# A two-block network on one core: the last gate's second half split into 160 and 96 columns

## The reference, cut to what matters

```python
def second_block(x, p, ...):
    ...
    for i in range(2):
        h = h + mix
        h = h + swiglu(rms_norm(h, norm_ffn[i]), ffn_w_in[i], ffn_w_out[i])
        gate = jax.nn.sigmoid(rms_norm(h, ple_norm[i]) @ ple_w_gate[i])
        h = h + gate * (p[i] @ ple_w_proj[i])
    return h
```

## Time and profile before

| | |
|---|---|
| runs, median (lowest to highest) | 1030.18 us (1029.44 to 1030.19) |
| the profiled execution's own time | 1030.42 us |
| its span, first to last instruction | 1028.5 us |
| TensorE busy in the span | 1021.3 us, 99% |
| VectorE, ScalarE, GpSimd busy | 84%, 64%, 7% |
| granted TensorE clock, mean | 1.000 |
| last matmul record starts | 1024.64 us |
| last transfer issued | about 1026.4 us |

### The profile page before, as it was taken

One profiled execution on the slowest core, in us unless ns is written; L12 is line 12 of the kernel. 1 busy time (PEld: TensorE's weight loads), 2 busy tenths in 40 slices (PEclk: granted clock), 3 DMA queues, 4 the chain that ended last, 5 costly groups with the idle time before them and its releaser, 6 DMA issues.

```text
span 1028.5 us, 17536 instructions
## 1 busy us (share of the span) xinstructions
PE 1021.3 (99%) x7069; PEld 934.7 (91%) x7069; DVE 861.6 (84%) x1072; ACT 657.4 (64%) x800; POOL 70.9 (7%) x53
## 2 busy tenths in 40 slices
PE   8999999999999999999999999999999999999998
PEld 8998999889999999888999999989888899999987
DVE  6888887689999978965899998777989699888874
ACT  5777545567666667765765656476876667555654
POOL 0000001200000030002005600010000200000010
PEclk9999999999999999999999999999999999999999
DMA  8746354655666646455465756555425466556651
GB/s 296 243 170 204 125 184 145 192 187 187 196 202 205 202 146 206 147 181 174 164 205 165 229 169 216 200 167 167 164 83 164 133 201 209 170 199 205 201 169 42
DMA packets 126657, 185.46 MB, mean 180 GB/s; under 512 B 3184, under 2 KB 97904, under 8 KB 126576
## 3 DMA queue, kind: packets, MB, share of 16 engines
q1 hardware_dynamic: 125984, 183.27, 54.0%
q0 software_dynamic: 160, 0.52, 0.2%
q10 hardware_dynamic: 432, 0.53, 0.2%
HBM read 183.26 MB, written 1.05 MB: 179 GB/s over the span
## 4 chain that ended last, share of the span: by engine, by line
PE 97%; DVE 1%; DMA 1%; issue 0%; ACT 0%; SPq 0%; DVEq 0%
PE PS L511 95%; PE PS L519 2%; DMA RAW<-in_w_in_dram 1%; DVE WL L2141 0%; DVE SC L2968 0%; DVE AR L2990 0%; DVE XT L3017 0%; SPq L3186 0%; DVE AR L2963 0%; DVE Z L3025 0%; DVE AR L2956 0%; DVE SC L2999 0%; ACT AR L1948 0%; DVE AR L2893 0%; ACT WH L1430 0%
## 5 line engine op out<-in xcount | busy, mean ns | idle before, releaser
L511 PE MATMUL PS<-Z,WH 128*128 128x256 f32 (+1 forms) x2608 | 484.4, 288 | 2.2 <-ACT WH L1430 1.7
L511 PEld LDWEIGHTS PS<-Z,WH 128*128 128x128 f32 x2608 | 407.8, 191 | 7.8 <-issue 1.6
L2134 DVE TENSOR_TENSOR WL<-RAW,WH 128x2048 fp32r<-128x2048 f32 (+4 forms) x174 | 354.1, 2041 | 51.1 <-ACT WH L1430 50.4
L511 PE MATMUL PS<-Z,WL 128*128 128x256 f32 x1352 | 370.9, 284 | 0.0
L511 PE MATMUL PS<-WH,Z 128*128 128x512 f32 (+1 forms) x1226 | 355.9, 366 | 0.3
L1430 ACT ACTIVATE WH<-RAW 128x2048 fp32r<-128x2048 f32 (+4 forms) x183 | 314.0, 1719 | 63.8 <-PE PS L511 52.5
L511 PEld LDWEIGHTS PS<-Z,WL 128*128 128x128 f32 x1352 | 255.5, 191 | 2.7
L511 PEld LDWEIGHTS PS<-WH,Z 128*128 128x128 f32 x1226 | 220.7, 189 | 37.1 <-issue 3.1
L511 PE MATMUL PS<-WL,Z 128*128 128x512 f32 (+1 forms) x613 | 222.2, 363 | 0.0
L511 PEld LDWEIGHTS PS<-WL,Z 128*128 128x128 f32 x613 | 116.0, 189 | 15.0
L511 PE MATMUL PS<-Z 128*128 128x512 f32 (+1 forms) x388 | 93.2, 388 | 0.0
(11 more groups left out here) (219 smaller groups left out, 766.1 us busy)
## 6 DMA issues: line engine op xcount, KB each, us to landing
RAW<-in_ffn_w_in_dram SPq DMA_DIRECT2D x44, 1024.0 KB, 5.2
RAW<-in_w_ff_dram SPq DMA_DIRECT2D x32, 1024.0 KB, 5.4
RAW<-in_ffn_w_out_dram SPq DMA_DIRECT2D x22, 1024.0 KB, 5.0
RAW<-in_w_in_dram SPq DMA_DIRECT2D x18, 1024.0 KB, 5.4
RAW<-in_gla_w_in_dram SPq DMA_DIRECT2D x12, 1024.0 KB, 5.3
RAW<-in_diff_w_in_dram SPq DMA_DIRECT2D x12, 1024.0 KB, 5.2
RAW<-in_ple_w_gate_dram SPq DMA_DIRECT2D x8, 1024.0 KB, 5.2
RAW<-in_w_out_dram SPq DMA_DIRECT2D x4, 1024.0 KB, 5.1
```

The source lines that it names most:

```text
L511: return e.matmul(o, l, r, start=start, stop=stop, skip_group_check=skip)
L2134: e.tensor_tensor(low, raw, high.bitcast(F32), ALU.subtract).then_inc(s["w_lo"], 1)
```

## The change

The second token block's last gate, 256 columns into bank 7, is made in two pieces: columns 0 to 159 into bank 7, then columns 160 to 255 into bank 3. The second piece waits for `ple_g` 5. Each piece has its own eight steps of three matmuls, its own sigmoid, its own product and sum, and its own transfer; the final wait is for six landings. The table `LAST_GATES` has a row for each piece: token block, first and last column, bank. Token block 0 stays whole.

```diff
+LAST_GATES = ((0, 0, 256, 6), (1, 0, 160, 7), (1, 160, 256, 3))
...
-        for tb in range(2):
+        for tb, n0, n1, bank in LAST_GATES:
+            if bank == 3:
+                e.wait_ge(s["ple_g"], 5)
             for k in range(8):
-                i = mm3(PS[:, 6 + tb, 0:256], [x[:, k, 128 * tb:128 * tb + 128] for x in ops],
-                        [x[:, k, :] for x in w], k == 0, k == 7)
-            i.then_inc(s["ple_t" if tb == 0 else "gemm"], 1)
+                i = mm3(PS[:, bank, 0:n1 - n0], [x[:, k, 128 * tb:128 * tb + 128] for x in ops],
+                        [x[:, k, n0:n1] for x in w], k == 0, k == 7)
+            i.then_inc(s["gemm" if bank == 3 else "ple_t"], 1)
...
-            for tb in range(2):
-                e.wait_ge(*((s["gemm"], c + 4) if tb else (s["ple_t"], 1)))
-                act(g[:, tb, 768:1024], PS[:, 6 + tb, 0:256], ACT.Sigmoid, scale=r[:, tb:tb + 1]).then_inc(s["ple_g"], 1)
+            for x, (tb, n0, n1, bank) in enumerate(LAST_GATES):
+                e.wait_ge(*((s["gemm"], c + 4) if bank == 3 else (s["ple_t"], x + 1)))
+                act(g[:, tb, 768 + n0:768 + n1], PS[:, bank, 0:n1 - n0], ACT.Sigmoid,
+                    scale=r[:, tb:tb + 1]).then_inc(s["ple_g"], 1)
...
-            for tb in range(2):
-                gated(8 + tb, tb, 768, 256)
+            for x, (tb, n0, n1, _) in enumerate(LAST_GATES):
+                gated(8 + x, tb, 768 + n0, n1 - n0)
...
-    for b in range(2):
-        e.wait_ge(s["ple_h"], 8 + b)
-        e.dma_start(o_rows[:, b, 768:1024], H[:, b, 768:1024]).then_inc(s["d_out"], 16)
-    e.wait_ge(s["d_out"], 80)
+    for x, (b, n0, n1, _) in enumerate(LAST_GATES):
+        e.wait_ge(s["ple_h"], 8 + x)
+        e.dma_start(o_rows[:, b, 768 + n0:768 + n1], H[:, b, 768 + n0:768 + n1]).then_inc(s["d_out"], 16)
+    e.wait_ge(s["d_out"], 96)
```

## The result

The changed kernel took 1032.12 us (median of 22 runs, 1031.11 to 1034.19), the kernel before 1030.21 us (22 runs, 1029.40 to 1032.23). The ratio is 1.0017, with a 95% interval of 1.0011 to 1.0023: 1.9 us by the medians, a small loss that the interval keeps apart from nothing. The forecast was 1032.0 us, plus 1.8. The profiled execution has a span of 1029.8 us; it reached the two pieces 0.53 us earlier than the profiled one before did, so times after 1021 us are compared as distances, not as they stand.

What follows compares the result with a forecast made beforehand. TensorE, busy 1021.3 of 1028.5 us, and the 3.56 us tail were taken as the bound. Plus 2.50 on TensorE less 0.68 in the tail gave plus 1.8 on 1030.18: 1032.0 us, range 1031.3 to 1032.8.

Steps and rivals of the forecast that it cites:

- TensorE's part: Matmuls of the two pieces: 48 at 0.112 us, 5.38 us instead of 2.88, so plus 2.50 us on the path.
- the last matmul's way through the array: Tail term: the last matmul, 160 columns narrower, passes through the array faster, minus 0.07 us.
- floor: Under every matmul on TensorE: its weight load sets at least 0.112 us, whatever columns it moves; given 65%.
- The tail: Last matmul, sigmoid, product, sum and transfer shrink by 160 columns: minus 0.68 us together, range minus 0.53 to minus 0.97.
- The wait: Second piece's wait for `ple_g` 5: the sigmoid it needs begins about 13 us earlier, so it costs nothing.
- the first piece's chain: First piece's sigmoid, product, sum and issue: under 1.65 us, hidden behind the second piece's 2.69 us of matmuls.
- the sixth transfer: The added transfer from splitting: the first piece's, 1.8 us at most, lands before the last one does, costing nothing.
- TensorE stays without gaps, so I leave the clock alone.: TensorE in the two pieces: granted clock stays at 1.00, the level of 2.4 GHz, so no clock cost was counted.
- By columns: Rival on TensorE: matmuls take 80 and 53 ns, minus 0.37 us, 1029.8 us; 12% together with a quicker float32r load.
- float32's pace: Rival on TensorE: float32r matmuls under 256 columns run as slowly as plain float32, 1037.3 to 1038.6 us; 17%.
- load and stream one after the other: Rival on TensorE: short streams can't cover the next load, pieces take 7.94 us, total 1034.6 us; 6%.
- quicker for float32r than for float32: Rival on TensorE: a quicker float32r weight load, result between by-columns and the forecast; 12% together with by-columns.

Runs made afterwards that it cites:

- half_load: The changed kernel, but its 96-column matmuls load 64 columns of weights instead of 128: 1030.88 us against 1030.23 for the kernel before.
- pe_only: Kernel before with only the matmuls split into 160 and 96 columns, both in bank 7, no wait, sigmoid to transfer whole: 1032.87 us against 1030.03.
- chain_only: Kernel before with its matmuls whole; only sigmoid, sums and transfer behind them in pieces of 160 and 96 columns: 1030.36 us against 1030.03.
- three_pieces: Kernel before with the second block's last gate in pieces of 96, 96 and 64 columns, banks 7, 4 and 3: 1037.46 us against 1030.23.
- both_blocks: The changed kernel with the first token block's last gate also split into 160 and 96 columns: 1034.76 us against 1030.23 for the kernel before.

## Why the prediction was right, step by step

- **TensorE's part, plus 2.50, and the last matmul's way through the array, minus 0.07.** The sum, 2.43, was found as 2.42. The parts are not as put: the last matmul's start and the sigmoid's are as far apart as before (1026.85 - 1026.54 = 0.31 against 1024.96 - 1024.64 = 0.32 in the earlier trace rows), so the 0.07 of the narrower matmul isn't at the end. The same amount shows where the width changes: the step behind the first matmul of each new width is 0.075 and 0.081 us in place of 0.112, 0.07 less in the two. That it came out equal was not foreseen. Step and floor were right, 0.112 for both widths, and `half_load` ties them to the load. The last matmul, forecast near 1027.1 us, started at 1026.54; 0.53 of that is the earlier arrival.
- **The tail.** Sigmoid minus 0.13, product and sum minus 0.33, as worked out. The transfer saved 0.2 us where 0.15 was taken, inside the bounds of 0 and 0.44.
- **The wait, the first piece's chain, the sixth transfer: nothing.** `pe_only` and `chain_only` bear it out.
- **"TensorE stays without gaps, so I leave the clock alone."** The outcome was right here, the reason was not. In `three_pieces` TensorE has no gaps either, and the clock halves. The changed kernel ends on 24 matmuls of 96 columns, and its profile keeps 1.00 up to the last; only in the 3.0 us behind it is the mean 0.80. How near it is to the fall, the other runs tell in part. An estimate from the rounded means: the changed kernel's 22 runs have 0.999 or 1.000, at most 3.1 us at 0.50, and 3.2 us lie behind its last matmul's start, so none need have lost the clock earlier. But one of nine runs of `pe_only`, with the same 48 matmuls on TensorE, has 0.997 and took 1034.10 us, 1.2 over the median of that kernel: at least 5.1 us at 0.50, where 3.9 lie behind the last matmul's start. One of five of `both_blocks` has 0.997 too (1035.66 us), and the 240 and 16 split lost the clock in its last two matmuls. So that the clock cost nothing here was in part luck. The prediction had no rival for this.
- **The rivals.** By columns (1029.8), float32's pace (1037.3 to 1038.6) and load and stream one after the other (1034.6) each had steps of their own, and none of these is in the trace: 160 and 96 columns have one step. Nor is a load seen that is quicker for float32r than for float32: the step is 0.111 us with float32r and 0.112 with the one-column float32 matmuls. The Trainium skill ("TensorE: Matmul & The Clock Gate", Weight-path perf modes — Fast Weight Load (FWL) and DoubleRow) has the quick load on when the number of weights is 128 and the dtype is not FP32; nothing in this trace shows it on for float32r.
- **The chances.** 48% within 0.2% and 50% slower was an even call on a mean of plus 1.8 with the bound at 2.06. The forecast's range ended at 1032.8; its own terms, 1032.5 and 0.4, make 1032.9. The ratio's interval, 1.0011 to 1.0023, still holds the bound.

## What to carry to other kernels

Cutting the last piece of a kernel to shorten its tail can pay only while each matmul still moves enough columns to cover its own weight load. Where 0.42 ns a column plus 13 ns reaches 0.112 us, that is at some 236 columns here, an estimate from the rows at 256 and 512. Below that the price is the number of matmuls times the load's step: here 48 x 0.112 us in place of 24 x 0.120, plus 2.5, for a tail that gave back 0.67. Read the floor from the narrowest matmuls with a full load in the trace before splitting. And look at the granted clock of a row of narrow matmuls even when TensorE is never idle: its fall can cost more than the instructions, and the wide matmuls behind pay too.

## What the runs showed of the hardware that was not expected

- A TensorE without idle time can lose its clock. In `three_pieces`, with 96 and then 64 columns a matmul, it went from 1.00 to 0.50 in the second piece; with 160 columns in each of the 72 it did not.
- At the lower level the step of 64-column and of 256-column matmuls is the same, 0.213 us. For 64 columns that is the load's floor, up from 0.112, so the load slows down with the clock (1.9 times). For 256 columns the stream at half the rate of 0.42 ns a column would come to 0.213 as well, and no run tells which of the two holds them.
- Moving columns that nobody reads made the kernel in three pieces 2.7 us faster (1037.46 to 1034.74). It stayed 4.5 us behind the kernel before.
- The time from the last matmul's start to its reader is 0.31 to 0.32 us with 256, 160 or 96 columns at the full clock and a load of 128; with the load of 64 and 96 columns it is 0.26 us, shorter by the 54 ns by which the load's record is shorter.
